# RWKV projections of a two-layer block as three rounded products, keys ahead of the low-rank gates, the context's rows finished ahead of the latents'

## The chip, the cores and the metric

The kernel runs on one core of one Trainium2 chip, with its engines TensorE (PE in the profile), VectorE (DVE), ScalarE (ACT), GpSimd (POOL) and SyncE (SP), which issues nearly all DMAs. The metric is the device time of one execution in microseconds (us), as the median of several runs.

## What is computed

Two transformer-like blocks follow each other on 256 latent tokens of width 1024. The second block has 256 context tokens beside them, and its last layer mixes with RWKV-7. The change is in that layer's projections:

```python
def rwkv_project(h, shifted, mu, w_rkv, w0, w1, w2, a0, a1, a2, g1, g2, kvec):
    xx = shifted - h
    xr, xw, xk, xv, xa, xg = (h + xx * mu[i] for i in range(6))
    r = xr @ w_rkv[0]
    k = xk @ w_rkv[1]
    v = xv @ w_rkv[2]
    lw = jnp.einsum("zblr,zrd->zbld", jnp.tanh(jnp.einsum("bld,zdr->zblr", xw, w1)), w2) + w0[:, None, None, :]
    decay = jnp.exp(-jnp.exp(-jax.nn.softplus(-lw.astype(jnp.float32)) - 0.5))
    a = jax.nn.sigmoid(a0 + (xa @ a1) @ a2)
    g = jax.nn.sigmoid(xg @ g1) @ g2
    kk = to_heads(k * kvec[0], RW_HEADS).astype(jnp.float32)
    kk = kk / jnp.maximum(jnp.sqrt(jnp.sum(kk * kk, axis=-1, keepdims=True)), 1e-12)
    k = k * (1 + (a - 1) * kvec[1])
    return {"r": r, "k": k, "v": v, "a": a, "g": g, "decay": decay, "kk": kk}
```

It is applied to context (`seq_shift`: neighbours in the sequence) and latents (`grid_shift`: neighbours in a grid of 4 x 64), whose `h` is a normalised and modulated residual. Everything is float32. The receptance `r` and the gate `g` are wanted for latents alone, since the layer has no context output.

## The kernel before

Every engine has its own program, in which the order is written out by hand: `rwkv_pe`, `rwkv_act`, `rwkv_dve`, and for the feed-forward before them `ffn_pe`, `ffn_act`, `ffn_dve` with i = 4. They meet in semaphores (`signal`; `kw_hi((1, 2))` counts one up, `kw_hi[1, 2]` waits for it). An engine takes its instructions strictly in order.

Weights come in pieces of 128 x 2048 (1 MB) into a ring of five slots. `tile_plan` (line 199) lists them in order of loading; SyncE issues them in that order, each when its slot's last user is through (`w_free`). The RWKV matrices are twelve pieces `("rkv", i, j)`, i = 1 keys, 0 receptance, 2 values, and a piece serves two tiles of 128 output features. The low-rank weights `ra1`, `ra2`, `rw1`, `rg1` go through the ring too.

Elsewhere in the kernel a float32 product is made in split form: ScalarE rounds the weights to the single-pass type ("high", `split_act`, into `w_high`), VectorE writes the remainder over the raw weights (`ring_low`), the same is done with the inputs (`x_both`), and TensorE adds three single-pass products:

```python
        def products(o, l, r, a, z):
            return [(o, l[0], r[0], a, False), (o, l[0], r[1], False, False), (o, l[1], r[0], False, z)]
```

The RWKV projections don't use it: `feature` (line 3428) multiplies float32 by float32, eight matmuls (one for each block c of 128 input features) for a tile k of 128 output features, 512 columns (256 context, 256 latent tokens) or 256 for receptance.

The stage in order. The down-projection of the feed-forward (i = 4, halves n, groups g of up to four blocks, four blocks tb of 128 tokens, of which 0 and 1 are context) ends it. `gates_end` (line 1877) finishes both residuals, then `norm_pe` turns context (`RAW[0]`) and latents (`RAW[1]`) by matmuls against a scaled diagonal; `row_high` on ScalarE writes the eight turned blocks of each into `XT`. VectorE makes the differences `XX` and the mixes XT + XX * mu, each into `XM` or `XMH` (areas of `wide`). TensorE's order is: low-rank 4 (the first factor of `a`, fed block by block), its second factor `ra2`, the keys' tiles 0 to 7 with head sums of their squares (`head_sums`), low-rank 1 (decay) and 5 (gate) between them, receptance with the broadcast of the inverse roots (`kb`), then the values without a pause. Behind stand the decay matmuls with `rw2` and the turns of the values.

## Time and profile before

| what | us |
|---|---|
| median of three runs | 2938.62 |
| lowest and highest | 2932.46, 2940.72 |
| the profiled execution | 2936.99 |
| its span | 2935.2 |

The span is cut here into stages by the first and the last instruction of each. The stretch between the end of the down-projection (2028.2) and the first decay matmul (2233.26) is 205.1 us. A float32 matmul stands in the trace as two records; a single-pass one as one record. A record's time reaches past the start of the next, so pace is read from starts. "ring_low", "w_high" and "x_both" are the parts of split products; "wide,ring" are the RWKV projections. The granted clock (PEclk) is a share of 2.4 GHz.

### The profile page before, as it was taken

The numbers are of one execution on the slowest core, as the hardware profiler recorded it, in microseconds if no ns is written. First come the engines' busy times: TensorE is split into PE (matmuls) and PEld (weight loads), VectorE is DVE, ScalarE is ACT, GpSimd is POOL, SyncE is SP. The second block draws the span as 40 slices with busy tenths as digits, with TensorE's granted clock in tenths as the row PEclk, the third lists the DMA queues.
The fourth block names the chain that finished last, engine by engine and source line by source line (L and its number), as shares of the span: only waits on it lengthen the run. The fifth ranks groups of instructions, "written<-read, shape, count | busy, mean of one in ns | idle before, by whom it ended". The sixth has DMA issues, their size and how long they took to land.

```text
span 2935.2 us, 58366 instructions
## 1 busy us (share of the span) xinstructions
PE 2744.0 (93%) x24236; PEld 2195.7 (75%) x24236; DVE 1714.5 (58%) x2670; ACT 1307.3 (45%) x2108; POOL 109.9 (4%) x152
## 2 busy tenths in 40 slices
PE   8999999999999999998888999998998888877998
PEld 7887788888877888677667877776454776764986
DVE  6756567577565775312566777644442564565885
ACT  6645566465565665322343522334212544433333
POOL 0000000000000000000000000000000232320000
PEclk9999999999999999997998999999998999998999
DMA  6554445555543554542001344331210000003443
GB/s 259 187 186 161 144 146 190 190 178 183 190 168 115 180 181 150 200 158 89 2 3 52 117 150 151 114 115 47 93 58 29 4 4 25 4 4 115 158 146 112
DMA packets 50390, 349.40 MB, mean 119 GB/s; under 512 B 5840, under 2 KB 5840, under 8 KB 9808
## 3 DMA queue, kind: packets, MB, share of 16 engines
q1 hardware_dynamic: 49680, 343.56, 32.7%
q8 instruction: 193, 3.16, 0.4%
q0 software_dynamic: 448, 2.11, 0.2%
q14 instruction: 69, 0.57, 0.1%
HBM read 344.61 MB, written 1.05 MB: 118 GB/s over the span
## 4 chain that ended last, share of the span: by engine, by line
PE 78%; DVE 13%; ACT 4%; issue 3%; DMA 1%; DVEq 0%; POOL 0%; ACTq 0%; SPq 0%; POOLq 0%
PE psum L170 76%; DVE arena L98 3%; DVE ring_low L87 2%; PE psum L175 2%; DVE arena L87 2%; DVE wide L87 1%; ACT wide L138 1%; ACT w_high L144 1%; DVE ring L87 1%; DVE wide L98 1%; ACT arena L144 0%; ACT arena L140 0%; DVE arena L94 0%; ACT L138 0%; DVE small L106 0%
## 5 line engine op out<-in xcount | busy, mean ns | idle before, releaser
L170 PE MATMUL psum<-x_both,w_high 128*128 128x512 f32 (+1 forms) x2800 | 843.6, 373 | 9.7 <-DVE arena L87 7.8
L87 DVE TENSOR_TENSOR ring_low<-ring,w_high 128x2048 fp32r<-128x2048 f32 (+3 forms) x254 | 560.2, 2206 | 428.6 <-ACT w_high L144 413.9
L144 ACT ACTIVATE w_high<-ring 128x2048 fp32r<-128x2048 f32 (+3 forms) x254 | 469.5, 1848 | 531.5 <-PE psum L170 236.5
L170 PE MATMUL psum<-x_both,ring_low 128*128 128x256 f32 (+1 forms) x2104 | 604.3, 301 | 0.0
L170 PEld LDWEIGHTS psum<-x_both,w_high 128*128 128x128 f32 x2800 | 493.8, 189 | 107.1 <-issue 18.4
L170 PE MATMUL psum<-w_high,x_both 128*128 128x512 f32 (+2 forms) x1440 | 453.4, 391 | 10.6 <-issue 10.0
L170 PEld LDWEIGHTS psum<-x_both,ring_low 128*128 128x128 f32 x2104 | 397.7, 189 | 32.0 <-DVE x_both L98 0.8
L170 PE MATMUL psum<-wide,ring 64*64 64x64 f32 (+3 forms) x2864 | 322.9, 298 | 13.1 <-issue 6.7
L170 PEld LDWEIGHTS psum<-w_high,x_both 128*128 128x128 f32 x1440 | 278.0, 197 | 74.9 <-issue 20.7
L170 PEld LDWEIGHTS psum<-wide,ring 64*64 64x64 f32 (+2 forms) x2864 | 206.3, 152 | 120.8 <-issue 97.0
L170 PE MATMUL psum<-ring_low,x_both 128*128 128x512 f32 (+2 forms) x720 | 279.3, 388 | 0.0
L144 ACT ACTIVATE arena<-psum 128x256 f32<-128x256 f32 (+1 forms) x341 | 148.4, 435 | 208.7 <-PE psum L170 181.4
L98 DVE SCALAR_TENSOR_TENSOR arena<-arena,prm 128x256 f32<-128x256 f32 x396 | 192.1, 485 | 14.1
L170 PE MATMUL psum<-w_high,h_high 128*128 128x512 f32 x440 | 172.3, 392 | 4.1 <-DVE ring_low L87 4.1
L170 PE MATMUL psum<-w_high,h_low 128*128 128x512 f32 x440 | 171.4, 389 | 0.0
L170 PE MATMUL psum<-ring_low,h_high 128*128 128x512 f32 x440 | 171.3, 389 | 0.0
L87 DVE TENSOR_TENSOR arena<-arena,psum 128x256 f32<-128x256 f32 (+1 forms) x240 | 112.3, 468 | 84.2 <-ACT arena L144 62.7
L170 PEld LDWEIGHTS psum<-ring_low,x_both 128*128 128x128 f32 x720 | 141.7, 197 | 24.9
L170 PE MATMUL psum<-ring 64*64 64x64 f32 x3072 | 116.6, 229 | 28.8 <-issue 11.2
L144 ACT ACTIVATE ring<-psum 128x256 f32<-128x256 f32 x256 | 98.1, 383 | 99.4 <-PE psum L170 81.9
L170 PEld LDWEIGHTS psum<-ring 64*64 64x64 f32 x3072 | 96.5, 139 | 43.1 <-issue 20.2
L170 PE MATMUL psum<-wide 64*64 64x64 f32 (+3 forms) x4016 | 111.0, 225 | 17.4 <-issue 6.9
(195 smaller groups left out, 3037.8 us busy)
## 6 DMA issues: line engine op xcount, KB each, us to landing
ring<-in_f_gu SPq DMA_DIRECT2D x88, 1024.0 KB, 4.8
ring<-in_w_mod SPq DMA_DIRECT2D x48, 1024.0 KB, 5.0
ring<-in_fu SPq DMA_DIRECT2D x44, 1024.0 KB, 4.9
ring<-in_f_dn SPq DMA_DIRECT2D x40, 1024.0 KB, 4.8
ring<-in_w_in SPq DMA_DIRECT2D x28, 1024.0 KB, 4.7
ring<-in_fd SPq DMA_DIRECT2D x20, 1024.0 KB, 4.9
ring<-in_rkvr SPq DMA_DIRECT2D x12, 1024.0 KB, 4.9
ring<-in_w_out SPq DMA_DIRECT2D x8, 1024.0 KB, 4.8
```

The costliest lines, as they stand in the source:

```text
L87: self.done(self.eng.tensor_tensor(o, a, b, op), then)
L98: self.done(self.eng.scalar_tensor_tensor(out=o, in0=a, scalar=s, in1=b, op0=op0, op1=op1), then)
L138: self.done(self.eng.activation(o, i, f, bias=bias, scale=scale), then)
L144: self.done(self.eng.activation(o, i, ACT.Copy, scale=scale), then)
L170: ins = self.eng.matmul(o, l, r, start=a, stop=z)
L175: ins = self.eng.transpose(o, i, ident[0:i.shape[0], 0:i.shape[0]])
```

## The change

Keys, receptance and values go in split form. `rkv_high` and `x_parts_high` (ScalarE) round weights and mixes, `rkv_low` and `x_parts_low` (VectorE) write the remainders, and `feature_step` issues three products where `feature` had one matmul. The rounded weights have places of their own (`HIGH_AT`, for keys' pieces 0 and 1 and for the values) or stand in the ring's slots 2 and 3 (`HIGH_SLOTS`), which so carry no loads meanwhile; eleven pieces share slots 0, 1 and 4, and the values' piece 1 has slot 2. Keys' pieces 0 and 1 are split during the last down-projection. The low-rank weights leave the ring: `ra1` and `rw1` for spare places of `wide`, `rg1` and `ra2` for `hc`, whose context rows have then been turned; the `ra1` load waits for the last of these turns.

TensorE takes keys 0 to 3 at once, block by block of the input, in four banks, then low-rank 4, and the other keys with low-rank 1 and 5 among them; the a-gate follows all keys. ScalarE therefore keeps the keys from PSUM in SBUF (`keys_act`, three passes of a tile where there were two), and VectorE scales them there (`key_block`). The last half of the down-projection does groups 4 and 5 for the context's blocks first (`down_steps`), and the context's gate, residual and squares move up with it. The turned blocks use two sets of four banks (`FB`, `OB`) for context and latents alike, where each of the eight blocks had a bank of its own; ScalarE's order of the rows is `RAW_ROWS`. The broadcasts `kb` and `unit_keys` move from receptance to the values.

```diff
 def tile_plan(dr):
...
-    plan.append((("ra1",), dr["ra1"], 512))
-    plan.append((("ra2",), dr["ra2"], 1024))
     for i in (1, 0, 2):
         for j in range(4):
             plan.append((("rkv", i, j), dr["rkvr"][i, j], WS))
-            if i == 1 and j < 2:
-                name = ("rw1", "rg1")[j]
-                plan.append(((name,), dr[name], 1024))
+            if i == 1:
+                for name in ((), ("ra1",), ("rw1",), ("rg1", "ra2"))[j]:
+                    plan.append(((name,), dr[name], APART[name]))
...
+HELD_OUT.update({("rkv", 1, j): i for j, i in enumerate((4, 0, 1, 4))})
+HELD_OUT.update({("rkv", 0, j): i for j, i in enumerate((0, 1, 4, 0))})
+HELD_OUT.update({("rkv", 2, j): i for j, i in enumerate((1, 2, 0, 1))})
+HIGH_SLOTS = {("rkv", 1, 2): 2, ("rkv", 1, 3): 3, ("rkv", 0, 0): 2, ("rkv", 0, 1): 3, ("rkv", 0, 2): 2, ("rkv", 0, 3): 3}
+BEHIND_HIGH = {("rkv", 2, 1): ("rkv", 0, 2), ("rw2", 0): ("rkv", 0, 3)}
...
+        SMALL_AT = {"ra1": wide[:, 24576:25088], "rw1": wide[:, 32000:33024], "rg1": hc[:, 0, :], "ra2": hc[:, 1, :]}
...
+        FB, OB = (6, 7, 2, 3), (0, 1, 4, 5)
+        RAW_ROWS = ([(RAW[0], k) for k in range(4)]
+                    + [(q, k) for n, p in ((0, ()), (2, (4, 5)), (4, (6, 7)))
+                       for q, ks in ((RAW[1], (n, n + 1)), (RAW[0], p)) for k in ks] + [(RAW[1], k) for k in (6, 7)])
...
+            if q in RAW:
+                return FB[k] if k < 4 else OB[k - 4]
...
+        def down_steps(i, n, tbs):
+            if (i, n) != (4, 1):
+                return [(g, tbs) for g in range(6)]
+            return [(g, tbs) for g in range(4)] + [(g, tbs[2 * j:2 * j + 2]) for j in range(2) for g in (4, 5)]
...
+                    if i == 4 and n and g in (3, 4):
+                        if g == 3:
+                            se.wait_ge(*hl_ok[4, 8])
+                        rkv_high(A, 1, g - 3)
...
+                    if i == 4 and n and g in (3, 4):
+                        rkv_low(D, 1, g - 3)
...
+        def rkv_high(A, i, j):
+            if (i, j) in HIGH_AFTER:
+                A.eng.wait_ge(*HIGH_AFTER[i, j])
+            A.eng.wait_ge(*landed(("rkv", i, j)))
+            A.copy(rkv_high_at(i, j), rkv_raw(i, j), kw_hi((i, j)))
+        def rkv_low(D, i, j):
+            D.eng.wait_ge(*kw_hi[i, j])
+            D.tt(low(("rkv", i, j)), rkv_raw(i, j), rkv_high_at(i, j).bitcast(F32), ALU.subtract, kw_lo((i, j)))
+        def x_parts_high(A, i, cs=range(8)):
+            for c in cs:
+                A.eng.wait_ge(*kx_ok[i, c])
+                A.copy(PXH[i][:, c, :], PX[i][:, c, :], kx_hi((i, c)))
+        def x_parts_low(D, i, cs=range(8)):
+            for c in cs:
+                D.eng.wait_ge(*kx_hi[i, c])
+                D.tt(PXL[i][:, c, :], PX[i][:, c, :], PXH[i][:, c, :].bitcast(F32), ALU.subtract, kx_lo((i, c)))
...
-                T.mm(bank(k % 4)[:, 0:cols], w[:, o:o + 128], x[:, c, :], c == 0, c == 7,
-                     None if c < 7 else w_free(key) if k % 2 else rw_mm(("rkv"[i], k)))
+            mms(T, products(bank(FB[k % 4])[:, 0:cols], [y[:, o:o + 128] for y in (rkv_high_at(i, k // 2), low(key))],
+                            [PXH[i][:, c, :], PXL[i][:, c, :]], c == 0, c == 7), then)
...
         def rwkv_pe(T):
             te = T.eng
             for q in RAW:
                 norm_pe(T, q)
+            for j in TWO:
+                te.wait_ge(*kw_lo[1, j])
+            for k in FOUR:
+                T.bank(FB[k], rw_act["kk", k])
+            for c in range(8):
+                te.wait_ge(*kx_lo[1, c])
+                for k in FOUR:
+                    feature_step(T, 1, k, c)
             low_rank(T, 4)
+            feature(T, 1, 4, rw_act["kk", 4])
+            head_sums(T, 0)
+            feature(T, 1, 5, rw_act["kk", 5])
+            head_sums(T, 1)
+            low_rank(T, 1)
+            feature(T, 1, 6, rw_act["kk", 6])
+            head_sums(T, 2)
+            feature(T, 1, 7, rw_act["kk", 7])
+            head_sums(T, 3)
+            low_rank(T, 5)
...
         def rwkv_act(A):
...
+            for n, (q, k) in enumerate(RAW_ROWS[3:]):
+                row_high(A, q, k)
+                if q == RAW[1] and k > 1:
+                    x_parts_high(A, 1, (k - 2,))
+            x_parts_high(A, 1, (6, 7))
+            rkv_high(A, 1, 2)
...
             A.act(small[:, 216:217], ident[:, 0:1], ACT.Sqrt)
             se.wait_ge(*rw_mm["kk", 7])
+            A.act(ROOTS, bank(4)[0:16, :], ACT.Sqrt, rw_act(("root", 0)))
+            x_parts_high(A, 2)
+            for k in range(8):
                 se.wait_ge(*tile_done(0, k))
+                A.copy(R[:, k, :], bank(FB[k % 4])[:, 0:256], rw_act(("r", k)))
+                if k == 1:
+                    rkv_high(A, 0, 2)
+                elif k == 3:
+                    rkv_high(A, 0, 3)
+                elif k == 5:
+                    rkv_high(A, 2, 0)
+            rkv_high(A, 2, 1)
...
         def rwkv_dve(D):
...
+            for c in range(8):
+                if c % 2 == 0 and c:
+                    context_shift(D, c // 2)
+                latent_shift(D, c)
+                mix_block(D, 2, PX[1], c, kx_ok((1, c)))
+                if c:
+                    x_parts_low(D, 1, (c - 1,))
...
             ve.wait_ge(*rw_act["root", 0])
             D.tsc(ROOTS, ROOTS, 1e-12, None, ALU.max, None)
             D.recip(ROOTS, ROOTS, rq_ok(0))
+            for k in FOUR:
+                key_block(D, k)
+            rkv_low(D, 0, 2)
+            x_parts_low(D, 2)
+            rkv_low(D, 0, 3)
+            for k in range(4, 8):
+                key_block(D, k)
+            rkv_low(D, 2, 0)
+            rkv_low(D, 2, 1)
```

TensorE, from the last down-projection matmul, before: turns, low-rank 4, then `ra2` and keys as one row.

```order
L170 MATMUL psum<-wide,hc 128x128 x16
L170 MATMUL psum<-wide,h 128x128 x16
L170 MATMUL psum<-wide,ring 64x512 x8
L170 MATMUL psum<-wide,ring 128x512 x40
L170 MATMUL psum<-wide,cx 16x512
L170 MATMUL psum<-wide,ring 128x512 x8
```

The same place after the change; `xk_high` and `xkv_low` are the parts of the keys' mix, `wk_high` the rounded piece 0 of the keys' weights.

```order
L170 MATMUL psum<-arena,hc 128x128 x16
L170 MATMUL psum<-arena,h 128x128 x16
L170 MATMUL psum<-xk_high,wk_high_64 128x512
L170 MATMUL psum<-xkv_low,wk_high_64 128x512
L170 MATMUL psum<-xk_high,ring_low 128x512
```

The turns are followed by split keys in place of the low-rank matmuls.

VectorE around the reciprocal of the roots, before: key blocks stand ahead of it, mixes and receptance copies (`hc<-psum`) behind it.

```order
L94 TENSOR_SCALAR wide<-wide,prm,small 128x512
L87 TENSOR_TENSOR wide<-wide,psum 128x512
L92 TENSOR_SCALAR wide<-wide 16x512
L115 RECIPROCAL wide<-wide 16x512
L98 SCALAR_TENSOR_TENSOR wide<-wide,prm 128x512 x8
L102 COPY hc<-psum 128x256 x2
L87 TENSOR_TENSOR wide<-wide,psum 128x512
L87 TENSOR_TENSOR wide<-wide 128x512
```

After the change, past the reciprocal; three more pairs like the first two rows stand between it and them.

```order
L94 TENSOR_SCALAR wide<-wide,prm,small 128x512
L87 TENSOR_TENSOR wide<-wide 128x512
L87 TENSOR_TENSOR ring_low<-ring,ring_low 128x2048
L87 TENSOR_TENSOR xkv_low<-wide,xv_high 128x512 x8
L87 TENSOR_TENSOR ring_low<-ring,ring_low 128x2048
L94 TENSOR_SCALAR wide<-wide,prm,small 128x512
```

Between reciprocal and unit keys stand now the key blocks, four remainders of weights and the remainders of the values' mix.

ScalarE from the root on, before: receptance copies, then values.

```order
L138 ACTIVATE wide<-psum,prm 128x512 x8
L138 ACT_TABLE_LOAD
L138 ACTIVATE small<-cst 128x1
L138 ACTIVATE wide<-psum 16x512
L144 ACTIVATE hc<-psum 128x256 x4
L144 ACTIVATE wide<-psum 128x512 x4
L138 ACT_TABLE_LOAD
```

The same place after it.

```order
L138 ACTIVATE wide<-psum 16x512
L144 ACTIVATE xv_high<-wide 128x512 x8
L144 ACTIVATE hc<-psum 128x256 x2
L144 ACTIVATE ring_low<-ring 128x2048
L144 ACTIVATE hc<-psum 128x256 x2
L144 ACTIVATE ring_low<-ring 128x2048
L144 ACTIVATE hc<-psum 128x256 x2
L144 ACTIVATE wv_high_62<-ring 128x2048
L144 ACTIVATE hc<-psum 128x256 x2
L144 ACTIVATE wv_high_63<-ring 128x2048
```

Rounded pieces of weights stand between the receptance copies, and the rounded mix of the values ahead of them.

## Rows read from the trace of the kernel before

**Rows 1.** Busy time by stretch: us, PE, PEld, DVE, ACT, POOL busy (x instructions), PEclk, DMA share, GB/s.
```profile
2047.20:2060.40 13.20, 9.45 (x17) 2.04 (x17) 11.94 (x25) 4.55 (x9) 0.00 (x0) 0.87 0.00 0
2052.00:2054.00 2.00, 2.00 (x4) 0.68 (x4) 1.75 (x4) 0.00 (x0) 0.00 (x0) 0.50 0.00 0
2177.20:2232.50 55.30, 55.23 (x130) 24.26 (x128) 8.05 (x15) 3.87 (x6) 0.00 (x0) 1.00 0.06 19
```

**Rows 2.** TensorE in order of time at the start: start, us, instruction, [idle before].
```profile
2027.79 0.39 PE L170 MATMUL psum<-w_high,x_both 128*128 128x512 f32 x1
2035.51 6.17 PE L170 MATMUL psum<-wide,hc 128*128 128x128 f32 x32 [7.33 <-DVE wide L92]
2041.94 5.31 PE L170 MATMUL psum<-wide,h 128*128 128x128 f32 x32 [0.26 <-ACT wide L138]
2049.08 1.04 PE L170 MATMUL psum<-wide,ring 128*64 128x512 f32 x2 [1.83 <-DVE wide L98]
...
2060.41 1.09 PE L170 MATMUL psum<-wide,ring 64*128 64x512 f32 x2 [0.73 <-issue]
```

**Rows 3.** TensorE in order of time, keys' head sum to the first decay matmul.
```profile
2095.11 1.03 PE L170 MATMUL psum<-wide,cx 128*16 128x512 f32 x2
...
2141.37 17.53 PE L170 MATMUL psum<-wide,ring 128*128 128x256 f32 x80
2158.84 1.93 PE L170 MATMUL psum<-wide,cst 16*64 16x512 f32 x8
2160.70 3.72 PE L170 MATMUL psum<-wide,ring 128*128 128x256 f32 x16
...
2177.24 55.20 PE L170 MATMUL psum<-wide,ring 128*128 128x512 f32 x128
2233.26 1.09 PE L170 MATMUL psum<-ring,wide 64*128 64x512 f32 x2 [0.83 <-issue]
```

**Rows 4.** TensorE in order of time in the down-projection, 512 columns.
```profile
2001.27 0.62 PE L170 MATMUL psum<-w_high,x_both 128*128 128x512 f32 x2
...
2001.95 0.62 PE L170 MATMUL psum<-w_high,x_both 128*128 128x512 f32 x2
```

**Rows 5.** TensorE in order of time where rounded matmuls have 256 columns.
```profile
1154.93 0.40 PE L170 MATMUL psum<-x_both,w_high 128*128 128x256 f32 x2
1155.06 0.19 PEld L170 LDWEIGHTS psum<-x_both,ring_low 128*128 128x128 f32 x1
1155.17 0.28 PE L170 MATMUL psum<-x_both,ring_low 128*128 128x256 f32 x1
...
1155.29 0.40 PE L170 MATMUL psum<-x_both,w_high 128*128 128x256 f32 x2
```

**Rows 6.** Groups of instructions by shape: the splits of 1 MB pieces.
```profile
L87 DVE TENSOR_TENSOR ring_low<-ring,w_high 128x2048 fp32r<-128x2048 f32 x236 | 541.0, 2292 | 384.3 <-ACT w_high L144 370.0 <-DVE h_low L87 0.5
...
L144 ACT ACTIVATE w_high<-ring 128x2048 fp32r<-128x2048 f32 x236 | 452.7, 1918 | 481.8 <-PE psum L170 200.0 <-DMA ring<-in_fu 161.6 <-DMA ring<-in_evt 65.6
```

**Rows 7.** VectorE and ScalarE in order of time.
```profile
2046.52 0.69 DVE L87 TENSOR_TENSOR wide<-wide 128x510 f32<-128x510 f32 x1 [0.42 <-ACT wide L138]
...
2059.31 11.84 DVE L98 SCALAR_TENSOR_TENSOR wide<-wide,prm 128x512 f32<-128x512 f32 x15
...
2142.94 3.34 DVE L115 RECIPROCAL wide<-wide 16x512 f32<-16x512 f32 x1
...
2041.33 10.44 ACT L138 ACTIVATE wide<-psum,modT,modD 128x256 f32<-128x256 f32 x16
```

**Rows 8.** DMA issues: count, KB each, median us to landing.
```profile
ring<-in_rkvr SPq DMA_DIRECT2D x12, 1024.0 KB, 4.9
```

**Rows 9.** Two waits of 3.26 us and the clock of the 5 us around their ends.
```profile
841.57 1.17 PE L175 MATMUL psum<-cst,arena 128*128 128x128 f32 x8 [3.26 <-DVE arena L87]
...
270.00:275.00 5.00, 1.74 (x12) 1.31 (x11) 4.69 (x6) 2.18 (x3) 0.54 (x1) 1.00 0.59 210
840.00:845.00 5.00, 3.44 (x14) 2.99 (x15) 4.55 (x8) 1.24 (x3) 0.00 (x0) 0.74 0.48 187
```

More of the change, by code:

```diff
@@ L380, in raw @@
         def raw(key):
+            if key[0] in APART:
+                return SMALL_AT[key[0]]
             return ring[:, slot_of[key], 0:width[key]]
@@ L899, in ffn_pe @@
             for n in range(2):
-                for g in range(6):
+                for g, blocks_here in down_steps(i, n, tbs):
                     key = ("dn", i, n, g)
@@ L2871, in program @@
[L2871 to L2875 removed]
+        RKV = [(i, j) for i in (1, 0, 2) for j in FOUR]
@@ new lines, in program @@
+        kw_hi, kw_lo = [signal(n, RKV) for n in ("kw_hi", "kw_lo")]
+        kx_ok, kx_hi, kx_lo = [signal(n, [(i, c) for i in (1, 0, 2) for c in range(8)]) for n in ("kx_ok", "kx_hi", "kx_lo")]
+        mix_ok = signal("mix_ok", [(4, k) for k in range(8)] + [1, 5])
+        n4_ok = signal("n4_ok", range(8))
+        rw_act = signal("rw_act", [("kk", k) for k in FOUR] + [("low", 4), ("kk", 4), ("kk", 5), ("low", 1), ("kk", 6), ("kk", 7),
+                                   ("low", 5)] + [("a", k) for k in range(8)] + [("root", 0)]
+                        + [("r", k) for k in range(8)] + [("v", k) for k in (0, 2, 4, 6)])
@@ L3516, in rows_out_pe @@
                          g == 0 and k == 0, g == 1 and k == 3, then)
-        def features(T, i, x, lo, done, taken_d, taken_a):
-            for k in range(8):
-                key = ("rkv", i, k // 2)
-                if k % 2 == 0:
-                    T.eng.wait_ge(*landed(key))
-                w = raw(key)
-                T.bank(k % 4, taken_a[k] if taken_a and k % 2 == 0 else taken_d[k])
-                for c in range(8):
-                    o = 256 * c + 128 * (k % 2)
-                    T.mm(bank(k % 4)[:, 0:512 - lo], w[:, o:o + 128], x[:, c, lo:512], c == 0, c == 7,
-                         None if c < 7 else w_free(key) if k % 2 else done(k // 2))
@@ L3574, in rwkv_act, with keys_act @@
             gate_root(A, ("r", 0))
+        def keys_act(A, k):
+            A.eng.wait_ge(*tile_done(1, k))
+            A.act(KK[:, k, :], bank(FB[k % 4]), ACT.Identity, scale=kv[:, 0, k:k + 1])
+            A.copy(K[:, k, :], bank(FB[k % 4]))
+            if k > 3:
+                A.eng.wait_ge(*rw_mm["kk", k - 4])
+            A.act(SQUARES[k % 4], bank(FB[k % 4]), ACT.Square, rw_act(("kk", k)), scale=kv[:, 0, k:k + 1])
         def low_act(A, i):
@@ L3592, in value_rows @@
                           p4[64 * cc:64 * cc + 64, 2 * u:2 * u + 2, :].rearrange("p v (i d) -> p i v d", i=2), then if u else None)
-        def mix(D, i, to, lo=0):
-            for k in range(8):
-                D.stt(to[:, k, :], XX[:, k, lo:512], mu[:, i, k:k + 1], XT[:, k, lo:512], ALU.mult, ALU.add,
-                      mix_ok(i) if k == 7 else None)
-        def receptance_block(D, k):
-            D.eng.wait_ge(*tile_done(0, k))
-            D.copy(R[:, k, :], bank(k % 4)[:, 0:256], rw_dve(("r", k)))
@@ L3636, in rwkv_dve @@
[L3636 to L3647 removed]
+            gate_end(D, GATES[3])
@@ new lines, in rwkv_dve @@
+            context_shift(D, 0)
+            norm_factors(D, RAW[1])
+            for c in range(8):
[5 more added lines that the diff above has]
+                    x_parts_low(D, 1, (c - 1,))
+            x_parts_low(D, 1, (7,))
+            for c in range(8):
+                mix_block(D, 4, XM[0], c, mix_ok((4, c)))
+            rkv_low(D, 1, 2)
@@ new lines, in rwkv_dve @@
+            ve.wait_ge(*w_free[("ra1",)])
+            for c in range(8):
+                mix_block(D, 1, XM[0], c, mix_ok(1) if c == 7 else None)
+            rkv_low(D, 1, 3)
+            rkv_low(D, 0, 0)
+            ve.wait_ge(*w_free[("rw1",)])
+            for c in range(8):
+                mix_block(D, 5, XMH[0], c, mix_ok(5) if c == 7 else None, 256)
+            for c in range(8):
+                mix_block(D, 0, PX[0], c, kx_ok((0, c)), 256)
+            ve.wait_ge(*w_free["rkv", 1, 3])
@@ L3648, in rwkv_dve @@
+            for c in range(8):
+                mix_block(D, 3, PX[2], c, kx_ok((2, c)))
+            x_parts_low(D, 0)
+            rkv_low(D, 0, 1)
             ve.wait_ge(*rw_act["root", 0])
```

265 lines of the change are left out of this document (133 added, 132 removed).

## The prediction

> **What bounds the kernel now.** I read the page's busy times first (TensorE is far ahead of the others), then the stages, then each engine in order of time. The change touches one stretch: from the last down-projection matmul of layer 0's feed-forward (start 2027.79, so done at 2028.2) [rows 2] to the first matmul behind the values (2233.26) [rows 3], and the 16 us before it. It is 205.1 us long. From 2060.4 on TensorE never stops, and VectorE and ScalarE mostly wait for it: in the values' 55.3 us VectorE works 8.05 us and ScalarE 3.87 [rows 1]. Ahead of 2060.4 the roles are swapped: TensorE waits 7.33 us for the context's scaled diagonal, then 1.83 us and less for mixed blocks [rows 2], while VectorE works 11.94 of 13.2 us [rows 1]. So TensorE's own time counts in full after 2060, and the chain over VectorE and ScalarE counts before it.
>
> **The matmuls.** A full-precision 128x512 matmul is two records; the values' 64 take 55.20 us, 0.8625 each [rows 3]. The change makes three rounded matmuls of each. Such ones stand in the down-projection: a group of three repeats from 2001.27 to 2001.95, 0.68 us [rows 4]. Keys and values have 64 each: 128 x (0.8625 - 0.68) = 23.4 us saved. Receptance has 64 of 256 columns: 40 of them run from 2141.37 to 2158.84, 0.437 each [rows 3]. Three rounded 256-column matmuls take 0.36 (1154.93 to 1155.29) [rows 5]: 64 x (0.437 - 0.36) = 4.9. TensorE's own saving is 28.3 us.
>
> A weight load is a record of 0.19 us, longer than the 0.12 between two such matmuls, so loads overlap there [rows 5]. If they didn't in the new code, a triple would be 3 x 0.19 = 0.57 and receptance would lose 8.5 us where I count 4.9 gained: a rival below. The Trainium skill, TensorE: Matmul & The Clock Gate, section Back-to-back issue gap, says that the spacing is set by both the load and the matmul; these rows show loads that cost nothing, and the measurement decides.
>
> **The start.** Down-projection groups 4 and 5 of the last half now run for the context's two blocks first. Of their 72 matmuls of 0.227 half is the latents', 8.2 us: the context is done at 2020.0. Its gate and residual (two multiplications, four additions, 0.7 to 0.79 each [rows 7]) and its squares then run beside TensorE. Behind 2028.2 remain VectorE's copy of the last block (0.7), the mean (0.37), ScalarE's root (0.2) and the diagonals (0.6), with hand-overs of 0.1: the context's transposes start at 2030.5, not 2035.51. The latents' gate, h (four of 0.79) and squares have less ahead of them: their transposes start at 2038.6, not 2041.94 [rows 2].
>
> A new wait takes this back. Latents' transposes 4 to 7 share PSUM banks with the context's 4 to 7, which ScalarE reads behind latents' rows 0 to 3 and the first rounded blocks of the keys' input. ScalarE takes 0.65 per row [rows 7] and some 0.63 per block (a quarter of the split's 1.92 and a fixed part [rows 6]). Followed through its new order, from latents' row 0 at 2040.0: context's row 4 at 2044.3, row 6 at 2049.6, the last transpose at 2051.0. TensorE idles 3.2 and 3.9 us there; only then do the keys' tiles 0 to 3 begin, block by block. VectorE has block 0 ready at 2043.7 and gives one every 2.65 us (shift 0.65, mix 0.79, low part 0.72, half a context shift of 0.93), the last at 2059.9. TensorE takes 4 x 0.68 = 2.72 per block, so it waits no more there: tiles 0 to 3 end at 2051.0 + 21.8 = 2072.8.
>
> **The rest, in TensorE's order.** After 2072.8: low-rank 4 and 1 (6.87 each) and 5 (3.45), the a-gate's eight (6.87), keys 4 to 7 (4 x 5.44) and eight head sums (0.93 each without the tail of the 1.03 [rows 3]; 7.5): 53.3 us, so 2126.1. The splits (2.29 on VectorE, 1.92 on ScalarE [rows 6]) fit in: the keys' weights 2 are in low form at 2068.6 and wanted at 2079.6, weights 3 at 2088.4 and wanted at 2099.3, receptance's 0 at 2098.0. A weight DMA takes 4.9 us [rows 8]; SyncE's queue is now held by the low-rank load until the context's transposes end (2036), and the keys' weights 2 behind it still land at 2042.
>
> Receptance is where the feed runs out: a tile of it is only 2.9 us, and a piece of weights serves two. VectorE waits for the root until 2129.0 (ScalarE needs all eight gates first, about 2127, and a table load), then does the reciprocal (0.45 + 3.34 [rows 7]) and four key blocks (1.31 each), and only then the low part of receptance weights 2: 2140.4, wanted at 2137.6. Behind it come eight low parts for the values (5.8), receptance weights 3 (2148.5), four key blocks (5.2) and the values' weights 0 (2156.1). TensorE stalls 3.0, 2.3 and 1.8 us: receptance is 23.0 + 5.3 and the values start at 2156.2. They take 43.5, the eight broadcasts 7.5: 2207.2. Their later weights are in time (2172.5 for 2181.7, 2185.2 for 2194.4). Last, the first decay matmul needs the bank of the last unit key, which VectorE leaves at 2208.7: 2208.9 in place of 2233.26, **24.4 us less**. Put the other way: 28.3 saved by the matmuls, less 3.9 by which waits grow (27.7 us of this stretch is neither these matmuls nor the other work of TensorE behind the transposes; after it is 22.8 + 7.1 + 1.7 = 31.6).
>
> **The clock.** In 2052 to 2054 the granted clock was 0.50, 1.2 GHz, though TensorE worked all of it [rows 1]: just before, it had worked in pieces with gaps of up to 1.83 us [rows 2]. After the change it works so from 2028 to 2051, so I expect the first keys' blocks at 1.2 GHz for some 4.5 us, of which half is lost: 2.3. The stalls of 2 to 3 us in receptance are like the stall of 3.26 us that ended at 841.57: 840 to 845 had 0.74, while after the same wait in 270 to 275 the clock stayed 1.00 [rows 9]. 0.26 of 5 us is 1.3, and nothing the other time; for three shorter stalls I take 0.9. Together 3.2, with bounds of 0 (nothing falls) and 8 (the keys 4 us, each stall 1.3). The Trainium skill, TensorE: Matmul & The Clock Gate, section What's actually happening, says that throttled is the default state and that activity releases it; by that a run of short pieces is the risk, as 2052 to 2054 shows.
>
> **Sum.** 24.4 - 3.2 = 21.2 us. The profiled execution took 2936.99 us (span 2935.2 and 1.79 around it), 1.63 under the median of the three runs, 2938.62. From its own time that is 2915.8, from the median 2917.4. I give 2917.
>
> **The rivals.**
> Feed worse than counted: rounding writes of 512 columns and key blocks in place are priced from neighbours. If VectorE and ScalarE take 15% more from 2129 on, the last low parts come 4 to 6 us later, the values' start with them, and the clock falls in each gap: gain 8 to 16, 2921 to 2930. For it: VectorE has no gap from 2129 to 2156. Against: its forms repeat to 1%.
> The clock holds and ScalarE's rows come quicker: gain 25 to 31, 2907 to 2913.
> Loads set the spacing: 0.57 per receptance triple takes 13.4 off the gain, 2930. [rows 5] speak against.
> Slower: TensorE stays at 1.2 GHz in the keys. If VectorE's pace per block goes over TensorE's 2.72 us (2.65 is close), each block ends in a gap, as in the low-rank stage now. Tiles 0 to 3 at half clock cost 21.8 more, the whole gain; from 30 us of matmuls at half clock, tiles 4 and 5 included, the kernel is slower by 9, 2947. Against: once fed, TensorE had 1.00 in all of the stages behind.
> The change doesn't do what it says: products as full-precision matmuls, three for one, would cost some 277 us more (128 x 2 x 0.8625 and 64 x 2 x 0.437). The rounded type of the same code in the down-projection rows and its 0.227 per matmul speak against.
>
> **How the numbers follow.** Forecast (gain 17 to 25, 2913 to 2922) 0.60; feed worse 0.16; clock holds 0.12; loads 0.04; slower 0.05; not as said 0.01; several small ones together, gain under 8, 0.02. The range takes the forecast, the clock's case and the poor feed, about 0.85, from 2907 to 2930. A difference under 0.3% (8.8 us) can't be told from none. Faster is 0.60 + 0.16 + 0.12 less 0.01 of the poor feed, 0.87; the same 0.07 (loads, small gains, that 0.01); slower 0.06.
>
> **What would show it.** Keys' tiles 0 to 3 as one piece of 22 to 24 us from about 2051; TensorE idle 3 to 4 us twice during the transposes; rounded triples of 0.68 and 0.36; three stalls in receptance released by VectorE's low parts, 7 us in all; none in the values; the first decay matmul 20 to 25 us earlier, waiting for VectorE; every later stage as long as before. I am wrong if low-rank or key tiles wait for a split, if triples are longer, or if a later stage changes.

## The result, and the profile after

The changed kernel takes **2949.27 us** (median of ten runs, 2942.91 to 2954.76) where the kernel before, on the same chip, takes 2938.39 (2932.46 to 2945.32): 1.0036 times as long, 95% interval 1.0023 to 1.005. It is slower, by 10.9 us, a small difference but clear of the noise; 2917 was forecast, 21 us faster. Its profiled execution took 2949.20 us, span 2947.4.

The stretch that was forecast did get shorter. TensorE's rows of the changed kernel in order of time (start, duration, operation, in brackets the idle time ahead of it and who ended it):

```profile
2025.55 3.85 PE L170 MATMUL psum<-arena,hc 128*128 128x128 f32 x32 [1.90 <-DVE arena L92]
2033.67 3.75 PE L170 MATMUL psum<-arena,h 128*128 128x128 f32 x16 [4.28 <-DVE arena L92]
2039.98 2.07 PE L170 MATMUL psum<-arena,h 128*128 128x128 f32 x8 [2.56 <-ACT wide L138]
2045.43 2.08 PE L170 MATMUL psum<-arena,h 128*128 128x128 f32 x8 [3.37 <-ACT wide L138]
2047.16 0.77 PE L170 MATMUL psum<-xk_high,wk_high 128*128 128x512 f32 x1
...
2070.16 1.07 PE L170 MATMUL psum<-wide 128*64 128x512 f32 x2
...
2139.89 0.39 PE L170 MATMUL psum<-xr_high,ring_low 128*128 128x256 f32 x1 [3.14 <-DVE ring_low L87]
2148.66 0.58 PE L170 MATMUL psum<-xr_high,ring_low 128*128 128x256 f32 x1 [2.75 <-DVE ring_low L87]
2156.61 0.47 PE L170 MATMUL psum<-xv_high,wv_high 128*128 128x512 f32 x1 [0.56 <-issue]
...
2211.61 1.09 PE L170 MATMUL psum<-ring,wide 64*128 64x512 f32 x2 [1.61 <-DVE wide L87]
2255.53 1.12 PE L170 MATMUL psum<-cx,wide 64*64 64x64 f32 x16 [0.66 <-DVE wide L87]
```

This execution stands 4.53 us ahead of the one before already in front of the change's stretch (its last down-projection matmul is at 2023.26 instead of 2027.79), so 4.53 is added to compare. That is scatter and nothing earned: the 10000th matmul record, in code that no edit touches, is at 1725.9 us before and at 1721.4 after, and in all profiles of this document it lies from 1717.9 to 1728.0. So single profiles are compared by stages, and whole kernels by medians. The first decay matmul is at 2211.61 instead of 2233.26 [rows 3]: 21.65 us earlier, of which the stretch earned 17.1. The last row is the first matmul of the scan (the recurrence over 16 chunks behind the projections). It stood at 2257.83 before: of 21.65 us only 2.3 are left 44 us later. Then the first part of the scan, up to the issue of the first output-weight load ("rwo", which SyncE gives out when a slot is free in mid-scan), takes 203.0 us instead of 189.9. SyncE's row of each kernel, before and after:

```profile
2447.73 0.33 SPq L3776 DMA_DIRECT2D ring<-in_rwo  x1
```

```profile
2458.51 0.33 SPq L3902 DMA_DIRECT2D ring<-in_rwo  x1
```

| difference to before, us | |
|---|---|
| ahead of the stretch | -4.5 |
| projections | -17.1 |
| decay stage (first decay to first scan matmul): 24.57 to 43.92 | +19.35 |
| scan's first part: 189.9 to 203.0 | +13.1 |
| rest | +1.4 |
| span | +12.2 |

So two stages that the change does not touch took 32 us more. TensorE's instructions are the same there in both kernels, in number, kind and order. What differs in the decay stage is seen in the busy time by stretch (stretch, its length, TensorE busy in it, records, granted clock, DMA share, GB/s); the kernel before:

```profile
2233.00:2243.00 10.00, 9.73 (x33) 1.00 0.28 105
2243.00:2253.00 10.00, 10.00 (x35) 1.00 0.00 1
```

and after:

```profile
2201.50:2211.50 10.00, 8.50 (x36) 1.00 0.00 0
2211.50:2221.50 10.00, 9.89 (x21) 0.59 0.00 0
2221.50:2231.50 10.00, 10.00 (x19) 0.50 0.00 1
2231.50:2241.50 10.00, 10.00 (x17) 0.50 0.01 2
2241.50:2251.50 10.00, 10.00 (x20) 0.50 0.00 0
```

The same stage runs at 2.4 GHz before and at 1.2 GHz after. The clock falls 1.7 us behind the end of the wait of 1.61 us, and stays down although the records fill every stretch.

### The profile page after: what moved, and what is told of

It reads as the page before. It is cut to its first block, busy times and chain, and to the rows that moved or that the text cites. A ratio compares the mean times of both kernels' runs of the same rounds, so it can differ in the third digit from the quotient of the medians.

```text
span 2947.4 us, 58912 instructions
## 1 busy us (share of the span) xinstructions
PE 2742.6 (93%) x24428; PEld 2229.9 (76%) x24428; DVE 1755.3 (60%) x2706; ACT 1352.3 (46%) x2157; POOL 107.8 (4%) x152
## 3 DMA queue, kind: packets, MB, share of 16 engines
q8 instruction: 195, 3.19, 0.4%
## 4 chain that ended last, share of the span: by engine, by line
PE 77%; DVE 14%; ACT 4%; issue 3%; DMA 1%; DVEq 0%; ACTq 0%; SPq 0%
PE psum L170 75%; DVE arena L98 3%; DVE ring_low L87 3%; PE psum L175 2%; DVE arena L87 2%; DVE wide L87 1%; ACT w_high L144 1%; DVE ring L87 1%; ACT wide L138 1%; DVE wide L98 1%; DMA ring<-in_evt 1%; ACT arena L144 0%; ACT arena L140 0%; DVE arena L94 0%; ACT ring L144 0%
## 5 line engine op out<-in xcount | busy, mean ns | idle before, releaser
L170 PE MATMUL psum<-w_high,x_both 128*128 128x512 f32 (+2 forms) x1440 | 451.4, 390 | 10.6 <-issue 10.1
L170 PE MATMUL psum<-wide,ring 64*64 64x64 f32 (+1 forms) x2416 | 157.3, 254 | 9.7 <-issue 6.6
L170 PEld LDWEIGHTS psum<-wide,ring 64*64 64x64 f32 (+1 forms) x2416 | 124.2, 146 | 32.7 <-issue 20.4
L170 PE MATMUL psum<-wide 64*64 64x64 f32 (+4 forms) x4048 | 125.9, 229 | 22.1 <-DVE ring L87 11.3
L170 PE MATMUL psum<-ring,wide 64*64 64x64 f32 (+2 forms) x2016 | 123.3, 251 | 13.5 <-issue 11.4
```

The source lines that it names most:

```text
L170: ins = self.eng.matmul(o, l, r, start=a, stop=z)
```

## Experiments

### The wait ahead of the decay stage

Theory 1: the wait ahead of the first decay matmul takes the clock, and the stage behind it, light in work for TensorE, cannot win it back. Theory 2: it is the values in split form that leave the clock about to fall. One experiment takes the wait away from the changed kernel, one puts it into the kernel before, one fills it.

`e1_banks`, in `rwkv_pe`, and the same in `rwkv_act`:

```diff
-                decay_item_pe(T, 0, tb, g, 4 + i % 4)
+                decay_item_pe(T, 0, tb, g, 4 + (i + 2) % 4)
```

> The changed kernel with one edit: the decay items take banks 6, 7, 4, 5 in turn instead of 4, 5, 6, 7, so the first one does not wait for the last unit key. Theory 1 (the 1.61 us wait of TensorE ahead of the decay stage makes the granted clock fall from 1.00 to 0.50, and this light stage cannot raise it): TensorE goes from the last broadcast to the first decay matmul without a wait, the clock stays 1.00 through most of the stage, and the stage from the first decay matmul to the first scan instruction is back from 43.9 us to 24 to 27 us; the kernel is 17 to 21 us faster than the changed one (2928 to 2932), and 28 to 34 us faster (2915 to 2921) if the scan's 13 us come from its slow start too. Theory 2 (the values in rounded form with the small broadcasts among them leave the clock about to fall whatever stands behind): the stage still takes 40 us or more, and only the 1.6 us of the wait are gained, 2947 to 2948.

`e2_before_wait`, in `rwkv_dve` of the kernel before:

```diff
+                if k == 7:
+                    D.copy(VT[:, k, :], bank(k % 4))
                 D.copy(VT[:, k, :], bank(k % 4), rw_dve(("v", k)))
```

> The kernel before with one added VectorE copy (the last value tile is copied twice, 0.7 us more), so that TensorE's wait ahead of the first decay matmul is 1.5 to 1.6 us instead of 0.83. Theory 1 (the wait alone makes the clock fall there): the decay stage goes from 24.6 to about 44 us in the kernel before as well, which is 15 to 21 us slower, 2953 to 2960, or up to 2972 if a slow start costs the scan 13 us more. Theory 2 (it takes what the change does ahead of it): 0.7 us slower, 2939.

`e3_fill`, in `rwkv_pe`, ahead of the wait for the last value tile:

```diff
+            for _ in range(7):
+                T.mm(bank(6), PXH[2][:, 0, 0:128], PXH[2][:, 0, :], True, True)
             te.wait_ge(*rw_dve["v", 7])
```

> The changed kernel with seven rounded 128x512 matmuls (0.227 us each, 1.6 us) added behind the last broadcast, into a bank that nobody reads, in the time in which TensorE waits for the last unit key: same order and banks, no idle time. Theory 1 (idle time makes the clock fall): the clock stays 1.00 in the decay stage, 24 to 27 us, and the kernel gains 17 to 33 us on the changed one (2916 to 2932), as with other banks. A rival to it (the order of the banks or the waits inside the stage make the difference, not the idle time): stage still above 40 us, 2948 to 2950.

The first without a wait (e1_banks), TensorE and its stretches:

```profile
2211.94 1.12 PE L170 MATMUL psum<-ring,wide 64*128 64x512 f32 x2
2236.53 0.68 PE L170 MATMUL psum<-cx,wide 64*64 64x64 f32 x16 [1.07 <-DVE wide L87]
```

```profile
2211.50:2221.50 10.00, 10.00 (x36) 1.00 0.00 1
2221.50:2231.50 10.00, 10.00 (x34) 1.00 0.01 2
```

The changed kernel with the wait filled (e3_fill):

```profile
2208.36 1.12 PE L170 MATMUL psum<-ring,wide 64*128 64x512 f32 x2
2232.96 0.68 PE L170 MATMUL psum<-cx,wide 64*64 64x64 f32 x16 [1.07 <-DVE wide L87]
```

The kernel before with the longer wait (e2_before_wait):

```profile
2236.11 1.15 PE L170 MATMUL psum<-ring,wide 64*128 64x512 f32 x2 [1.55 <-issue]
2280.76 1.12 PE L170 MATMUL psum<-cx,wide 64*64 64x64 f32 x16 [0.65 <-DVE wide L87]
```

```profile
2236.00:2246.00 10.00, 9.89 (x20) 0.55 0.23 93
2246.00:2256.00 10.00, 10.00 (x18) 0.50 0.00 0
```

One copy of 0.69 us on an engine that had nothing to do cost the kernel before 20.5 us: 2960.39 against 2939.89, ratio 1.0075 (1.0063 to 1.0087). The stage went from 24.57 to 44.65 us. In the changed kernel other banks brought it from 43.92 to 24.59, and the kernel to 2932.85, ratio 0.998 (0.9969 to 0.999). Filling gave 24.60 us in its profile, but 2942.34 as the median, ratio 1.0009 (0.9999 to 1.0019), where 2932 at most was expected. Its eleven runs go from 2932 to 2947 and the profile is of the fastest, so that I don't claim that the clock held in all of them; why the median is 9.5 us above that of e1_banks stays open. Theory 2 is out: split values stand ahead of the decay stage in e1_banks as well, and are absent in e2_before_wait. A wait of 0.83 us [rows 3] left the clock alone there, waits of 1.55 and 1.61 did not.

The gain of e1_banks on the changed kernel is 16.4 us by median, though (measured beside a kernel before of 2939.89 and 2938.39), not the 28 to 34 that I expected if the scan's loss hung on the clock: its scan took 204.4 us up to the load, after a start at 1.00. The scan's loss has a cause of its own.

### The scan: where blocks of instructions end

In the scan the long waits of the changed kernel are of a peculiar kind. TensorE between 2365 and 2369 (merged rows; sixteen matmuls that belong to one group are one row where nothing parts them):

```profile
2365.84 0.41 PE L170 MATMUL psum<-ring,wide 64*64 64x64 f32 x16
2366.14 0.24 PE L170 MATMUL psum<-ring 64*64 64x64 f32 x1
2368.10 0.40 PE L170 MATMUL psum<-ring 64*64 64x64 f32 x12 [1.73 <-issue]
2368.32 0.22 PE L170 MATMUL psum<-wide 64*64 64x64 f32 x1
2368.33 0.23 PE L170 MATMUL psum<-ring 64*64 64x64 f32 x3
```

A group of sixteen is broken open behind its first, with 1.73 us of nothing. A wait on a semaphore can't stand there: only the first of a group carries one. And no engine ends it, "issue" does. In the stretches around it there is one transfer:

```profile
2365.00:2366.00 1.00, 1.00 (x69) 1.00 0.06 16
2366.00:2367.00 1.00, 0.38 (x21) 1.00 0.00 0
2367.00:2368.00 1.00, 0.00 (x0) 1.00 0.00 0
2368.00:2369.00 1.00, 0.90 (x31) 1.00 0.00 0
```

The page lists queues of the kind "instruction", before and after:

```profile
q8 instruction: 193, 3.16, 0.4%
```

```profile
q8 instruction: 195, 3.19, 0.4%
```

195 packets of 3.19 MB are 16 KB each. TensorE has 24428 matmul and as many load records, and with the waits that stand alone its trace holds 49933 instructions, 256 a packet. Such breaks are 124 to 126 matmul records apart or a multiple of it (records 2830, 2955, 3080, 3205 and 3330 of the scan, for instance), which with their weight loads and waits is one packet. If the records of each trace are numbered from the start of the program, modulo 256, all 283 breaks of over 0.25 us that "issue" ends in this part of the scan, in the fourteen profiles of this document together, stand at the places 193 to 196, wherever the scan begins, and each ends 2.1 to 2.9 us after the start of the latest 16 KB transfer. So TensorE runs dry at the end of a block of 256 instructions, and goes on some 2.5 us after the next block's transfer began. The Trainium skill, Runtime: NRT & Kernel Launch, section Instruction fetch mechanics, says that blocks of 256 instructions are streamed in and that crossing one's end is mostly hidden; block and size agree, but here crossings showed, by up to 1.9 us in this kernel.

Why would the change matter? A scan round (both head groups, one chunk) is 1280 instructions three times running early in each half of the scan, 5 x 256 exactly, and later 1538, 6 x 256 + 2. The ends fall on the same steps round after round, so that good or bad luck is not averaged out; this last point is argued, since no run changes the length of a round. The change adds 385 instructions ahead of the scan (a full-precision matmul is two matmul and two load records, its three rounded ones are six, which is two more for each of 192; and a wait), which moves the scan's first matmul from place 147 of a block to place 20. Waits without work move it back.

`e5_pad`, in `rwkv_pe`:

```diff
             for q in RAW:
                 norm_pe(T, q)
+                if q == RAW[0]:
+                    for _ in range(255):
+                        te.wait_ge(ld_cst, 16)
```

> Adds nothing but instructions without work: the changed kernel with 255 more waits on a semaphore that has long been reached (127 instructions as built), in TensorE's stream ahead of the latents' transposes, where it waits 4.28 us anyway. Counted as the records show them (a load and a matmul record for each pass, and one for each wait of its own), TensorE's stream up to the first scan matmul is 24467 instructions in the kernel before and 24852 in the changed one; in blocks of 256 the scan begins at place 147 before and at place 20 after. With the 127 it begins at place 147 again. Block theory (in the scan TensorE runs out of fetched instructions at the ends of blocks, and where these ends fall within the scan's steps decides how much of each fetch is seen): the way from the first scan matmul to the issue of the first output-weight load goes from 203 us back to about 190, and the kernel is 10 to 13 us faster than the changed one, 2936 to 2939; the clock still falls in the decay stage. Rival (the scan is longer because of its clock, its start or its data): 203 us and 2947 to 2951.

`e6_before_pad`: 257 such waits in the kernel before, ahead of its context's transposes.

> The reverse: the kernel before with 257 such waits (128 instructions as built) ahead of the context's transposes, where TensorE waits 7.33 us anyway, so that its scan begins at place 19 of a block. Block theory: first part of the scan 190 to about 203 us, the kernel 10 to 14 us slower than before, 2949 to 2953. Rival (nothing but the work decides): 190 us and 2939 to 2941.

Time that TensorE's matmuls lost to "issue" in the scan's first part (us in total, times, longest), in this order: before, after, e5_pad, e6_before_pad:

```profile
PE psum L170 <- issue: 12.1, 18, 1.3
```

```profile
PE psum L170 <- issue: 20.8, 19, 1.9
```

```profile
PE psum L170 <- issue: 14.9, 19, 1.2
```

```profile
PE psum L170 <- issue: 22.7, 22, 1.8
```

These sums grow by 8.7 us with the change and by 10.6 with the 257 waits, where the stage itself grows by 13.1 and 12.3; the rest follows from them or is open. The two ends of the stage in e6_before_pad:

```profile
2254.37 0.68 PE L170 MATMUL psum<-cx,wide 64*64 64x64 f32 x16 [1.07 <-DVE wide L87]
```

```profile
2456.58 0.33 SPq L3778 DMA_DIRECT2D ring<-in_rwo  x1
```

The stage follows the place in a block at which the scan's first matmul stands, in all profiles:

| scan begins at place | first part, us |
|---|---|
| 147, 148 | before 189.9; e2_before_wait 191.4; e5_pad 191.5; e7_feed_pad 190.7; e9_two_cures 190.9; e10_all 189.2; e12_scan_fill 189.2 (148 behind its fill) |
| 19, 20, 33 | e6_before_pad 202.2; after 203.0; e1_banks 204.4; e4_feed 205.0; e3_fill 204.1 |
| 84 | e8_feed_pad64 195.0 |
| 212 | e11_all191 200.1 |

e6_before_pad computes what the kernel before does and took 2948.97 against 2941.13, ratio 1.0031 (1.0018 to 1.0044): 7.8 us by median, less than the 10 to 14 expected and than the 12.3 of the stage in its profile. The rival, that work and clock decide, is out: e2_before_wait starts its scan at 1.2 GHz and has 191.4, e1_banks starts at 1.00 and has 204.4, and the mean granted clock of the stage is 0.93 to 0.97 in every profile, 0.95 before and 0.96 in e6_before_pad.

The whole time of e5_pad missed the 2936 to 2939 expected: 2946.46, ratio 1.0004 (0.9981 to 1.0026). The waits cost more than I took: with 127 of them TensorE idled 12.93 us instead of 4.28 ahead of the latents' transposes, 0.1 us each, 8.65 us in the open. One of its twelve runs took 14755 us and stands apart from all others. The rest fall into two groups, 2925 to 2930 (four, mean clock 0.963 to 0.968) and 2937 to 2955 (seven, 0.955 to 0.960): the same wait of 1.60 us ahead of the decay stage seems to take the clock in some runs and not in others. The profile is of the second kind, and there is none of the first, so this is not shown.

### The feed

`e4_feed`: e1_banks, context's rows 4 and 5 read ahead of the latents' (`RAW_ROWS`), and in the receptance stage

```diff
-            for k in FOUR:
-                key_block(D, k)
+            x_parts_low(D, 2, (0, 1, 2))
             rkv_low(D, 0, 2)
-            x_parts_low(D, 2)
+            x_parts_low(D, 2, (3, 4, 5))
+            key_block(D, 0)
             rkv_low(D, 0, 3)
-            for k in range(4, 8):
-                key_block(D, k)
+            x_parts_low(D, 2, (6, 7))
+            key_block(D, 1)
             rkv_low(D, 2, 0)
+            for k in (2, 3):
+                key_block(D, k)
```

with key blocks 4 to 7 beside the values, and ScalarE's rounding of the values' input between its receptance copies.

> The changed kernel with the other banks of the first experiment, and two orders changed so that TensorE is fed in time: the context's rows 4 and 5 are read out of their banks before the latents' rows (TensorE idles 2.56 and 3.37 us there in the changed kernel), and in the receptance stage VectorE makes low parts before the key blocks, which go beside the values, and ScalarE rounds the values' input between the receptance tiles (stalls of 3.14, 2.75 and 0.56 us). The feed theory (these waits are what stood between 24.4 us and more): keys' tiles 0 to 3 end about 5.5 us earlier and receptance is 6 us shorter, so 10 to 12 us less than with the banks alone. The rival (VectorE's pace in the keys' input, 2.65 us per block, then leaves gaps that keep the clock at 0.50, and VectorE is full during the values): 0 to 5 us less than with the banks alone, or slower.

It took 2926.59, ratio 0.9957 (0.9945 to 0.9969), 6.3 less than the banks alone by median and 9.6 by the place of the first decay matmul (2202.31 against 2211.94); 10 to 12 was expected, so the feed theory is right in kind and a little too high. The receptance stalls are gone, TensorE has no wait above 0.5 us from 2046 to the decay stage; the transposes still wait 1.04 and 2.60 us. The rival's full VectorE did not come.

### Both causes taken away

`e7_feed_pad` and `e8_feed_pad64` are e4_feed with 255 and 129 waits (127 and 64 instructions) in the place of e5_pad.

> The best version so far (other banks for the decay items, both feed orders) with the same 127 instructions more, scan at place 147. Block theory: 205 us of scan become about 191, 12 to 14 us less than the 2926.6 of that version: 2912 to 2916. Rival: 2926 to 2928.

> The same version with 64 instructions instead of 127: the scan begins at place 84 of a block, which neither kernel has. Block theory: the scan's first part changes again, to somewhere from 188 to 208 us, the kernel to 2910 to 2930; stalls stand every 125 matmul records, 31 records away from where they are without the addition. Rival: no change, 2926 to 2928.

They took 2919.54 (ratio 0.993, 0.9914 to 0.9946) and 2921.24 (0.9935, 0.992 to 0.9949). The scan gave 14.3 and 10.0 us, but e7_feed_pad missed its 2912 to 2916: its waits took part of the gain back, TensorE idling 11.70 us ahead of the latents' transposes instead of 4.28 (4.80 in e8_feed_pad64). So the next kernels have them between the triples of keys and values, in `feature_step`:

```diff
+            for _ in range(2 * (i == 1) + 2 * (i == 2)):
+                T.eng.wait_ge(ld_cst, 16)
             mms(T, products(...
```

`e9_two_cures` has this (two waits, one instruction as built, for each of 128 triples) and e1_banks' edit, `e10_all` this and e4_feed's, `e11_all191` the same as e10_all with twice as many waits beside the values.

> The changed kernel with the two causes taken away and nothing else: the decay items take banks 6, 7, 4, 5 (no wait ahead of the decay stage), and 128 waits of TensorE on a semaphore that has long been reached, one between any two triples of the keys' and the values' matmuls (0.68 us each, so that a wait of some 0.1 us hides), which put the scan at place 148 of a block of 256 instructions, against 147 before and 20 in the changed kernel. Theory (the projections save what was forecast, and only the clock in the decay stage and the ends of fetch blocks in the scan took it back): first decay matmul 20 to 23 us earlier than before, decay stage 24.6 us, first part of the scan 190 to 192 us, the kernel 2916 to 2924. Rival (a third cause, such as the values' split form or the later scan): 2928 to 2935.

> The same with both feed orders (context's rows 4 and 5 read first; low parts ahead of key blocks in the receptance stage). In the run with 127 waits in one place, they took 0.1 us each and put off the latents' transposes by 8 us; between the triples they should cost nothing. Theory: 8 to 10 us less than the two cures alone, 2907 to 2914. Rival (0.1 us each shows between the triples too, 13 us): 2919 to 2924.

> The same with 192 added instructions, the scan at place 212 of a block. Block theory: the way from the first scan matmul to the issue of the first output-weight load differs from the 191 us of place 148 (20 gave 203 to 205, 84 gave 195), by at least 2 us either way, and the long issue waits stand 32 matmul records earlier in the stream. Rival (what counted was only a count of blocks, or chance): 190 to 192 us again.

e9_two_cures, TensorE at the decay stage and SyncE in the scan:

```profile
2207.30 1.12 PE L170 MATMUL psum<-ring,wide 64*128 64x512 f32 x2
```

```profile
2422.77 0.33 SPq L3904 DMA_DIRECT2D ring<-in_rwo  x1
2649.16 1.28 SPq L3904 DMA_DIRECT2D ring<-in_rwo  x3
```

It took **2920.36**, ratio 0.9935 (0.9923 to 0.9947), with decay stage 24.59 and scan part 190.9: 19.7 us less than the kernel before, near the 21 forecast for the change itself, once both causes are out. No third cause of their size is left. The agreement is in part luck: stage by stage the projections of e9_two_cures earn 19.0 us, but the second part of its scan takes 226.4 us instead of 221.7, which is among the open points at the end, and its profiled execution stood 7.0 us ahead of the one before by scatter. e10_all took 2913.58, 0.9909 (0.9896 to 0.9921), within the theory's range. e11_all191 took 2927.41, 0.9967 (0.9951 to 0.9984), 13.8 us more than e10_all; 10.9 of them are in the scan's first part, 200.1 instead of 189.2 at the same start (2228.19 and 2228.16). Two of its seven runs took 2940 and 2941, at a mean clock of 0.96 where the others have 0.963 to 0.966; why is open.

### The clock at the scan's start

`e12_scan_fill`: e10_all with eight idle full-precision matmuls in TensorE's first three waits of the scan (two, three and three), and the added waits beside half of the values' triples left out. Of its edit the filler alone is shown:

```diff
+        def idle(T, n):
+            for _ in range(n):
+                T.mm(bank(6)[:, 0:256], ident, cst[:, 0:256], True, True)
```

> The second of these four with eight full-precision 128x256 matmuls into a bank that nobody reads, 0.43 us each, in TensorE's first three waits of the scan (1.07, 1.62 and 1.32 us), and fewer added waits, so that behind them the scan stands at place 148 again. In every kernel so far the clock fell to 0.50 in or just ahead of these waits and was back some 20 us later. Clock theory: with the waits filled it stays at 1.00 or falls later and for less, and the first 22 us of the scan take 5 to 8 us less. Rival (the scan's short 64x64 matmuls are not enough whatever stands ahead of them): it falls all the same, within 1 us of the second, or 1 to 3 us slower.

The stretches from the scan's start in e10_all, then in e12_scan_fill:

```profile
2228.20:2233.20 5.00, 2.06 (x54) 0.66 0.01 3
2233.20:2238.20 5.00, 3.22 (x51) 0.50 0.00 0
2238.20:2243.20 5.00, 4.68 (x110) 0.50 0.01 3
2243.20:2248.20 5.00, 4.50 (x125) 0.97 0.02 3
```

```profile
2222.80:2227.80 5.00, 4.86 (x76) 1.00 0.01 3
2227.80:2232.80 5.00, 3.21 (x69) 0.87 0.00 0
2232.80:2237.80 5.00, 4.21 (x99) 0.50 0.01 3
2237.80:2242.80 5.00, 5.00 (x92) 0.61 0.01 3
```

The clock falls later and for some 10 us instead of 13.7, but the 5 to 8 us expected from it did not come: the scan's first part is 189.2 us in both, and the same wait for VectorE comes 27.5 us behind the start in one and 27.1 in the other. The median, 2910.41 (ratio 0.9902, 0.9886 to 0.9918), can't be told from e10_all's. The likely reason, which no run separates, is that waits on other engines set the pace there and a faster TensorE only waits longer. Both beat the kernel before, by 0.9 and 1.0%.

## Why the prediction was wrong

**The projections: right, 4 us short.** With 4.53 added, step by step (forecast, found): context's transposes start 2030.5, 2030.1; the latents' 2038.6, 2038.2; TensorE idles 3.2 and 3.9, found 2.56 and 3.37; keys' tiles 0 to 3 end at 2075.1 with the clock's loss, found 2074.7; stalls in receptance of 3.0, 2.3 and 1.8 behind low parts, found 3.14, 2.75 and 0.56, the first two ended by VectorE's writes of ring_low. What is missing is TensorE's own work. From 2156.61 to the first decay matmul it is 55.0 us where 52.7 stood in the sum: a value tile and its broadcast repeat every 6.67 us (2162.26, 2168.93), which leaves 1.23 us for a broadcast where 0.93 was counted, 2.4 us for the eight. From 2070.16 to receptance (2124.98) it is 54.8 where 53.3 was counted. The clock term was about right: 1.2 GHz was granted for 2.2 us at the keys' start and for 3.4 us in receptance, by estimate half of each lost, 2.8 us against 3.2. In all 17.1 us instead of 21.2.

**"Every later stage as long as before": this step was wrong, and it is nearly the whole miss.** It was written as a sign to look for, and carried the sum without a price: the terms for everything behind the first decay matmul were nothing, and the runs showed 32.5 us. Two things broke it.

First the **clock**. The prediction names the wait at this very place ("the first decay matmul needs the bank of the last unit key") and even has its size: TensorE is through at 2207.2 and goes on at 2208.9, 1.7 us, and 1.61 came. It charges these 1.7 us and nothing for the clock behind them. Its clock term, 3.2 with bounds of 0 and 8, covers keys and receptance alone, where dense matmuls of 512 and 256 columns stand behind each gap and the clock rises again: at the keys' start it was 1.00 after some 2 us; in receptance it stayed at 1.00 behind the stall of 3.14 us and was at 0.50 for 3.4 us behind that of 2.75 (mean 0.83 over 2145 to 2155). The stage behind this wait has only matmuls of 64 rows, small turns and one broadcast each, and it ran 44 us at 1.2 GHz. The term was too small by 19.35 us. The mechanism was even among the rivals, with a chance of 0.05, but in the keys, where it didn't happen; I asked where gaps are long and not what stands behind them. Before, 0.83 us at the same place [rows 3] had gone unpunished, which I took for a property of the stage.

Second the **instruction stream**. The change makes three rounded matmuls, six instructions with their loads, of one full-precision matmul, which is four; I counted their time and not their number. 385 instructions more moved every block end in the scan, for 13.1 us. Nothing in the sum had a term for it, and e6_before_pad shows that the number alone does it: the same work with 128 instructions more has the longer stage. The rows that could have warned are the breaks of 1.1 to 1.3 us "issue" in the scan of the kernel before and its 193 instruction packets.

**The rivals.** Feed worse than counted did not come: the stalls in receptance and ahead of the values are 6.5 us where 7.1 was counted. The clock did not hold. Loads never set the spacing: a receptance triple repeats in 0.36 us (2125.20, 2125.56, 2125.91). The products are what they should be. What the range lacked was a case in which the gain is earned and lost again further on: 2930 as its upper end takes no loss behind 2211 at all.

## What to carry to other kernels

A saved microsecond counts only if the stages behind keep their pace: price each new wait by the work that stands behind it, since a gap of 1.6 us ahead of a light stage cost 20 us, and two of 3.1 and 2.8 us ahead of dense matmuls cost under 2 us beside their own length. Where an engine issues thousands of small instructions in rounds of about a whole number of fetch blocks, adding or removing instructions anywhere ahead can change the time of the loop, here from 189 to 205 us; try a few paddings before a version is judged, and compare versions at the same place. A change that does less work and is not faster deserves a look at the stages that it does not touch.

## What the runs showed of the hardware

- With the clock down, TensorE's records filled 10 of 10 us for 40 us at 0.50. The Trainium skill, TensorE: Matmul & The Clock Gate, section What's actually happening, has it that activity releases the throttle; here full records and a clock that stayed down stand side by side, while at the keys' start, with 128x512 matmuls, it rose within some 2 us.
- At one and the same place a wait of 0.83 us left the clock at 1.00, waits of 1.55 and 1.61 us were followed by 0.50, and the runs with one of 1.60 us fell into two groups some 20 us apart. Length alone does not decide: in receptance a stall of 3.14 us left it at 1.00, and one of 2.75 us was followed by 3.4 us at 0.50.
- Waits that are fulfilled long ago cost TensorE's stream 0.08 to 0.1 us each when they stand together (128 instructions in an idle time of 9.86 us, 127 in 11.70 and 12.93), and nothing to be seen between matmul triples of 0.68 us (from the last down-projection matmul to the first decay matmul 186.5 us with them in e9_two_cures and without them in e1_banks).
- TensorE's instructions come in packets of 16 KB, 256 each, in the changed kernel's scan one in 4.6 us on average (3.6 to 6.3). Where TensorE ran dry it went on 2.1 to 2.9 us after the transfer's start, and what was left of this time at the block's end was idle time inside a group of matmuls.
- Open: the second part of the scan, from the first output-weight load to the next three, was 221.7 to 224.9 us in before, after, e2_before_wait and e5_pad, and 225 to 233 in the others, with places 147 and 19 or 20 in both groups. No run here separates what sets it.
